# Up projections of a conv feed-forward as 2x2 block products with seven products of block sums

## The reference

```
g, u = split(h @ w_up)               # 1024 -> 2 * 2816
y = (silu(dwconv3(g, w_conv)) * u) @ w_down
```

## Time and profile before

| | us |
|---|---|
| median of 3 runs | 1462.82 |
| lowest, highest | 1462.06, 1465.18 |
| span of the profiled execution | 1461.5 |
| PE busy | 1418.0 (97%) |
| DVE busy | 1003.8 (69%) |
| ACT busy | 521.3 (36%) |
| POOL busy | 85.7 (6%) |

### The profile page before, as it was taken

One profiled execution on the slowest core, in us unless ns is written; L12 is line 12 of the kernel. 1 busy time (PEld: TensorE's weight loads), 2 busy tenths in 40 slices (PEclk: granted clock), 3 DMA queues, 4 the chain that ended last, 5 costly groups with the idle time before them and its releaser, 6 DMA issues.

```text
span 1461.5 us, 20681 instructions
## 1 busy us (share of the span) xinstructions
PE 1418.0 (97%) x7952; PEld 1225.0 (84%) x7952; DVE 1003.8 (69%) x1537; ACT 521.3 (36%) x833; POOL 85.7 (6%) x139
## 2 busy tenths in 40 slices
PE   6999899999999999999999999989999999999998
PEld 3788698889888888888888878868998888888887
DVE  5587988778867666656665688788757555555555
ACT  4342866234222122222121225466445233223321
POOL 0023700000000000000000000350000000000000
PEclk9999999999999999999999999999999999999999
DMA  9643011332643243325333411301022322322324
GB/s 386 278 132 99 1 44 61 130 114 101 200 130 115 88 142 115 106 95 155 118 95 106 138 49 58 115 15 44 15 97 92 101 86 100 100 86 86 114 92 139
DMA packets 42983, 158.62 MB, mean 109 GB/s; under 512 B 5168, under 2 KB 6576, under 8 KB 41776
## 3 DMA queue, kind: packets, MB, share of 16 engines
q1 hardware_dynamic: 42928, 157.87, 32.3%
HBM read 155.76 MB, written 2.10 MB: 108 GB/s over the span
## 4 chain that ended last, share of the span: by engine, by line
PE 84%; DVE 9%; ACT 3%; DMA 2%; issue 1%; SPq 0%; DVEq 0%; ACTq 0%
PE ps L708 67%; PE ps L646 4%; PE ps L647 4%; PE ps L648 4%; DMA ada_step<-in_w_step 1%; DVE w_lo L1373 1%; DVE tmp L1473 1%; PE ps L858 1%; PE ps L660 1%; DVE H_lo L1482 1%; DMA w_raw<-in_w_main 1%; DVE nmax L1687 1%; DVE qn L1660 1%; DVE pt_lo L1488 1%; DVE part_sums L1635 1%
## 5 line engine op out<-in xcount | busy, mean ns | idle before, releaser
L708 PE MATMUL ps<-H_hi,w_hi 128*128 128x512 f32 (+1 forms) x1280 | 449.1, 351 | 4.2 <-DVE H_lo L1482 1.7
L708 PE MATMUL ps<-H_lo,w_hi 128*128 128x512 f32 (+1 forms) x1280 | 447.4, 350 | 0.0
L708 PE MATMUL ps<-H_hi,w_lo 128*128 128x512 f32 (+1 forms) x1280 | 447.1, 349 | 0.0
L1045 ACT ACTIVATE w_hi<-w_raw 128x1024 fp32r<-128x1024 f32 x180 | 187.5, 1055 | 423.3 <-PE ps L708 368.3
L708 PEld LDWEIGHTS ps<-H_hi,w_hi 128*128 128x128 f32 x1280 | 242.3, 189 | 38.3 <-DVE H_lo L1482 3.2
L708 PEld LDWEIGHTS ps<-H_hi,w_lo 128*128 128x128 f32 x1280 | 242.2, 189 | 31.6
L708 PEld LDWEIGHTS ps<-H_lo,w_hi 128*128 128x128 f32 x1280 | 242.3, 189 | 30.8
L1495 DVE SCALAR_TENSOR_TENSOR X<-ps,mod,X 128x512 f32<-128x512 f32 (+1 forms) x296 | 180.8, 644 | 108.5 <-PE ps L708 87.3
L1373 DVE TENSOR_TENSOR w_lo<-w_raw,w_hi 128x1024 fp32r<-128x1024 f32 x180 | 221.1, 1239 | 37.5 <-ACT w_hi L1045 36.4
L708 PE MATMUL ps<-inner_hi,w_hi 128*128 128x512 f32 (+1 forms) x528 | 187.6, 355 | 0.3 <-DVE X L1495 0.3
L708 PE MATMUL ps<-inner_lo,w_hi 128*128 128x512 f32 (+1 forms) x528 | 187.2, 355 | 0.0
(11 more groups left out here) (200 smaller groups left out, 1846.8 us busy)
## 6 DMA issues: line engine op xcount, KB each, us to landing
w_raw<-in_w_main SPq DMA_DIRECT2D x182, 512.0 KB, 3.3
ada_raw<-in_w_ada SPq DMA_DIRECT2D x73, 512.0 KB, 4.1
ada_step<-in_w_step SPq DMA_DIRECT2D x7, 2048.0 KB, 14.6
X<-in_x SPq DMA_DIRECT2D x2, 1024.0 KB, 6.8
cb<-in_cvec SPq DMA_DIRECT2D x2, 1024.0 KB, 7.3
out_x<-X SPq DMA_DIRECT2D x8, 256.0 KB, 4.6
rtab<-in_rope SPq DMA_DIRECT2D x4, 384.0 KB, 7.2
X<-in_ctx SPq DMA_DIRECT2D x2, 512.0 KB, 7.9
```

Of the source, the lines that this page charges most:

```text
L708: ins = pe.matmul(job.ps(a, b), ww[:, wsl], xx[:, xk, a:b], start=first and n == 0, stop=last and n == 2)
L1045: act.activation(w_hi[c % 4][:], w_raw[c % 2][:], ACT.Copy).then_inc(chunk_hi, 1)
```

## The change

Units 1 to 10 of the feed-forward compute their up projections in another way; unit 0 and all of `down` keep their products. The two feature tiles of the gate (and then the two of u) are taken as a 2x2 block product: 2 output tiles by 2 halves of the 1024 input features, times 2 halves of the features by 2 halves of the tokens (384 tokens in layer 0, 256 in layer 1). Instead of eight block products there are seven (Winograd's form), numbered 0 to 6 below; each is 4 feature blocks by three matmuls over half the tokens. A group of seven is called `pair`; a unit is the gate pair, `down` of the unit before, the u pair. In unit 10 both pairs stand before `down`.

Sums of token blocks are made once a layer: POOL adds `hi` and `lo` back together (`whole`, five instructions), DVE makes seven sums (`t_add`) and five `lo` tiles (`t_low`), ACT four `hi` tiles beside the one for `H` (`t_high`). Sums of weight blocks are made in place in the raw chunks by DVE, four of 512 columns for each pair (`weight_sum`), and weights are split in pieces of mostly 512 columns (`block_hi`, `block_lo`, a ring of six blocks).

The running sum of products 0, 2 and 4 stays in one PSUM slot. ACT copies it out after product 0, 2 and 4 (`snapshot`), and PE may not add the next product before that. DVE adds the other products to these copies (`add_part`: part 0 must be done before product 6, which goes over product 3 in PSUM). Taps, silu and value then work from SBUF (`gbuf`, `ubuf`). Loads come as two chunks at a time (`load_ff`, `w_ff`). The tables of layer 1 are loaded behind the feed-forward of layer 0, and three chunks of layer 1's first weights are split in its normalisation, where it were two.

```diff
+            def whole(dst, ks, a):
+                hi, lo = (x[:, ks, a:a + hw].bitcast(F32) for x in H)
+                pool.tensor_tensor(dst[:, :, 0:hw], hi, lo, ALU.add).then_inc(h_sum, 1)
+            Job(JOB["wo", L][15]).ready(pool)
+            pool.wait_ge(h_lo[nn], half(nn))
+            whole(u5_raw, slice(0, 4), 0)
+            whole(t4_raw, slice(4, 8), 0)
+            pool.wait_ge(h_lo[nn], half(nn) + 4)
+            whole(t3_raw, slice(0, 4), hw)
+            pool.wait_ge(h_lo[nn], half(nn) + KD)
+            for n in range(2):
+                whole(u6_raw[n], slice(4 + 2 * n, 6 + 2 * n), hw)
...
-            def up(jn, c, i):
-                for n in range(4):
-                    job = Job(jn + n, i, 24)
-                    pe.wait_ge(chunk_lo, c + n + 1 + 12 * i)
-                    job.open(pe)
-                    for one in turn_about(sg, n):
-                        for kk in range(KD):
-                            last = part(job, [one], slot(c + n), P * kk, H, kk, kk == 0, kk == KD - 1)
-                    job.filled(last)
...
+            def pair(un, z):
+                ab, cd = un.pair_jobs(L, z)
+                for b in range(PAIR):
+                    pe.wait_ge(fw_lo, FF_OPS * L + un.op(z, BLOCK_OP[b]))
+                    if b == 0:
+                        ab.open(pe)
+                    if b == 1:
+                        cd.open(pe)
+                        pe.wait_ge(t_lo, 5 * L + 4)
+                    if b == 2:
+                        pe.wait_ge(snap, 60 * L + un.at(6, 3 * z + 1))
+                    if b == 4:
+                        pe.wait_ge(snap, 60 * L + un.at(6, 3 * z + 2))
+                        pe.wait_ge(t_lo, 5 * L + 5)
+                    if b == 6:
+                        pe.wait_ge(c22, 20 * L + un.at(2, z + 1))
+                    job, o = ((ab, 0), (cd, 512), (ab, 0), (cd, 0), (ab, 0), (ab, 512), (cd, 0))[b]
+                    w = 512 * un.block(z, b)
+                    for r in range(4):
+                        for n, (wx, tx) in enumerate(((0, 0), (0, 1), (1, 0))):
+                            ins = pe.matmul(job.ps(o, o + hw), fw[wx][:, w + P * r:w + P * (r + 1)], operand(tx, b, r),
+                                            start=b in (0, 1, 3, 5) and (r, n) == (0, 0), stop=(r, n) == (3, 2),
+                                            skip_group_check=b in (2, 4, 6))
+                            if b >= 5 and (r, n) == (0, 0):
+                                job.filled(ins)
+                    ins.then_inc(prod, 1)
+            def down(jobs, blocks, ops, tiles, x):
...
+            def unit(un):
+                pair(un, 0)
+                if un.last:
+                    pair(un, 1)
+                down([un.down_job(L, m) for m in range(KD)], [un.down_block(k) for k in range(2)], un.down_op(1), un.at(2, 2), inner)
+                if not un.last:
+                    pair(un, 1)
...
+            def snapshot(un, z, n):
+                act.wait_ge(prod, 140 * L + un.at(14, 7 * z + 1 + 2 * n))
+                z_buf, src = (gbuf, ubuf)[z], un.pair_jobs(L, z)[0].ps(0, hw)
+                if n < 2:
+                    act.activation(z_buf[:, 0, hw * n:hw * (n + 1)], src, ACT.Copy).then_inc(snap, 1)
+                else:
+                    both = z_buf[:, 1, 0:w].rearrange("p (s c) -> p s c", s=2)
+                    act.activation(both, src.unsqueeze(1).to_broadcast([P, 2, hw]), ACT.Copy).then_inc(snap, 1)
+            def unit(un):
+                x, y = un.raw("G")
+                snapshot(un, 0, 0)
+                act.wait_ge(fw_sum, 80 * L + un.at(8, 4))
+                block_hi(un.block(0, 6), x[:, 512:1024])
+                snapshot(un, 0, 1)
+                down = un.raw("D")
+                un.landed(act, L, "D")
+                block_hi(un.down_block(0), down[0][:])
+                snapshot(un, 0, 2)
+                block_hi(un.down_block(1), down[1][:])
+                act.wait_ge(c22, 20 * L + un.at(2, 1))
+                tapped(1, un.at(2, 3), gbuf[:, 1, 0:w])
+                x, y = un.raw("U")
+                un.landed(act, L, "U")
+                act.wait_ge(prod, 140 * L + un.at(14, 6))
+                block_hi(un.block(1, 0), x[:, 0:512])
+                act.wait_ge(prod, 140 * L + un.at(14, 7))
+                block_hi(un.block(1, 1), y[:, 0:512])
+                un.pair_jobs(L, 0)[1].taken(act)
+                tapped(0, un.at(2, 2), gbuf[:, 0, 0:w])
+                for n, t in enumerate((1, 0)):
+                    act.wait_ge(taps, 80 * L + un.at(4 * len(sg), 2 * len(sg) * (n + 1)))
+                    silu(t, (1.0, -1.0)[t])
+                un.down_job(L, KD - 1).ready(act)
+                act.wait_ge(fw_sum, 80 * L + un.at(8, 7))
+                block_hi(un.block(1, 2), x[:, 0:512])
+                block_hi(un.block(1, 3), y[:])
+                block_hi(un.block(1, 5), x[:, 512:1024])
+                act.wait_ge(ff_lo[L], un.at(2, 2))
+                snapshot(un, 1, 0)
+                act.wait_ge(fw_sum, 80 * L + un.at(8, 8))
+                block_hi(un.block(1, 6), x[:, 512:1024])
+                x, y = un.raw("G next")
+                un.landed(act, L, "G next")
+                act.wait_ge(prod, 140 * L + un.at(14, 9))
+                block_hi(0, x[:, 0:512])
+                snapshot(un, 1, 1)
+                block_hi(1, y[:, 0:512])
+                snapshot(un, 1, 2)
+                act.wait_ge(fw_sum, 80 * L + un.at(8, 11))
+                block_hi(2, x[:, 0:512])
+                act.wait_ge(v_done, 20 * L + un.at(2, 1))
+                inner_hi(1, inner)
+                act.wait_ge(prod, 140 * L + un.at(14, 13))
+                block_hi(3, y[:])
+                act.wait_ge(prod, 140 * L + un.at(14, 14))
+                block_hi(5, x[:, 512:1024])
+                act.wait_ge(v_done, 20 * L + un.at(2, 2))
+                inner_hi(0, inner)
...
+            dve.wait_ge(h_sum, 5 * L + 5)
+            dve.wait_ge(t_sum, 7 * L + 1)
+            for n in range(2):
+                t_add(t3r[:, 2 * n:2 * n + 2], u6r[n], 1.0, t3r[:, 2 * n:2 * n + 2])
+            dve.wait_ge(t_sum, 7 * L + 3)
+            for n in range(2):
+                t_add(u6r[n], u6r[n], -1.0, u5r[:, 2 * n:2 * n + 2])
+            dve.wait_ge(t_sum, 7 * L + 5)
+            for n in range(2):
+                t_add(t4r[:, 2 * n:2 * n + 2], u6r[n], -1.0, t4r[:, 2 * n:2 * n + 2])
+            t_low(u5[1][:, :, 0:hw], u5r, u5[0][:, :, 0:hw], 1)
+            dve.wait_ge(t_sum, 7 * L + 7)
+            for n in range(2):
+                t_low(u6_lo[n][:, :, 0:hw], u6r[n], u6_hi[:, 2 * n:2 * n + 2, 0:hw], 2 + n)
+            t_low(t4[1][:, :, 0:hw], t4r, t4[0][:, :, 0:hw], 4)
+            def add_taps(t, tile, src, signal, done, count, last=None):
...
-                ff_value(t, u, c0 + C_FF + 4 + 2 * t, t, 0, 0, 0)
+                g, u = Job(JOB["u0", L] + 2 * t), Job(JOB["u0", L] + 2 * t + 1)
+                if L == 0:
+                    ada_u0(t)(0)
+                add_taps(t, t, g.ps(0, w), ff_conv[L], (2 * len(sg) - 1) * t, t + 1, g)
+                if t == 0:
+                    block_lo(0, x[:, 0:512], 1)
+                    block_lo(1, y[:, 0:512], 2)
+                    weight_sum(x, y, 1, 0, 0)
+                else:
+                    weight_sum(x, y, 1, 0, 2)
+                    block_lo(2, x[:, 0:512], 3)
+                    block_lo(3, y[:], 4)
+                if L == 0:
+                    ada_u0(t)(1)
+                u.ready(dve)
+                dve.wait_ge(ff_silu[L], t + 1)
+                u.last_read(dve.tensor_tensor(ubuf[:, t, 0:w], tmp[t][:, 0:w], u.ps(0, w), ALU.mult))
+                if t == 0:
+                    weight_sum(x, y, 1, 0, 1)
+                else:
...
+            def add_part(un, z, part):
+                z_buf, (ab, cd) = (gbuf, ubuf)[z], un.pair_jobs(L, z)
+                first, second = slice(0, hw), slice(hw, 2 * hw)
+                if part == 0:
+                    dve.wait_ge(snap, 60 * L + un.at(6, 3 * z + 3))
+                    dve.tensor_tensor(z_buf[:, 1, first], z_buf[:, 1, first], cd.ps(512, 512 + hw), ALU.add)
+                    dve.tensor_tensor(z_buf[:, 1, second], z_buf[:, 1, second], cd.ps(0, hw), ALU.add).then_inc(c22, 1)
+                elif part == 1:
+                    dve.wait_ge(prod, 140 * L + un.at(14, 7 * z + 6))
+                    ab.last_read(dve.tensor_tensor(z_buf[:, 0, first], z_buf[:, 0, first], ab.ps(512, 512 + hw), ALU.add))
+                else:
+                    dve.wait_ge(prod, 140 * L + un.at(14, 7 * z + 7))
+                    cd.last_read(dve.tensor_tensor(z_buf[:, 0, second], z_buf[:, 0, second], cd.ps(0, hw), ALU.add))
...
+            def unit(un):
+                x, y = un.raw("G")
+                block_lo(un.block(0, 6), x[:, 512:1024], un.op(0, 5))
+                ada_ff(un, 0)
+                down = un.raw("D")
+                for k in range(2):
```

(41 more changed lines are left out.)

552 lines of the change are left out of this document (389 added, 163 removed).

## The result

The changed kernel takes **1592.2 us** (median of 4 runs, 1591.18 to 1596.94) against 1463.0 of the kernel before in the same session (1462.06 to 1465.18): a ratio of 1.0885, 95% interval 1.0868 to 1.0902. It is slower, as forecast, but by 129 us and not by 81, and 2 us outside the range. The profiled execution has a span of 1589.6 us against 1461.5.

What follows compares the result with a forecast made beforehand. PE's instruction stream was taken to bound the kernel. On the 1461.5 us span, units (+7, +26), starts (+30, +6), unit 10 (+1.6, +4.6) and last downs (+5.4) summed to +81: 1544 us, range 1500 to 1590.

Steps and rivals of the forecast that it cites:

- PE's pace: Units 1 to 10: PE's own matmul time if it never waits, 45.9 us a unit in layer 0, 31.1 in layer 1.
- wait (1): Product 6 of the gate pair waits for the chain after product 4: 2.2 us in layer 0, 2.4 in layer 1.
- Wait (2): Product 2 of the next gate pair waits for DVE, then ACT's copy: 1.2 us in layer 0, 1.75 in layer 1.
- Layer 0's unit: Steady feed-forward unit of layer 0: 45.9 us of PE plus 4.9 of waits, 50.8; nine units cost +7 us.
- wait (3): Product 4 of the u pair waits for DVE's queue, with some at product 6: 1.5 us; layer 1 0.25.
- The clock falls: Rival, 18%: PE's waits lower its clock, 1.7 us once in each of 18 units, +31: 1575 us.
- The start of layer 0: Before unit 1: POOL's sums end at 348.5, then DVE's queue delays PE; costs 30 us, or 36 by POOL's slow row.
- The start of layer 1: Before unit 1: narrower tiles, no modulation; product 6 comes 6 us late (3 to 10).
- Layer 1's units: Steady feed-forward units of layer 1: 31.1 us of PE plus 4.4 of waits, 35.5; nine units cost +26 us.
- The ends: Unit 10 adds 1.6 us in layer 0 and 4.6 in layer 1; the last down 2.7 in each layer.
- Lighter waits: Rival, 17%: waits at product 2 of the gate pair and product 4 of the u pair vanish; 1502 us.
- PE goes at its own pace: Rival, 6%: copies ready in time, PE waits only at the starts (14 + 3 us) and ends (5.4): 1428 us.

Runs made afterwards that it cites:

- the last kernel: The one with the three edits, plus two layer 0 modulation columns moved into the normalisation and, in unit 10, one ACT copy before a tap: 1516.9 us.
- the one with the three edits: Changed kernel with part 0's additions ahead of the second down split, token-block sums on DVE, and ACT's copies earlier: 1518.9 us, ratio 1.0379.

## Why the prediction was wrong

The sign and most of the places were right; the size was 48 us short. Two steps failed: the clock was kept out of the sum, and POOL's additions were priced on POOL with nothing for DVE beside them.

- **PE's pace and wait (1)** stand as worked out. PE alone was put at 45.9 in layer 0, and 46.25 were measured where DVE didn't hold it. Product 6 starts 2.29 us (layer 0) and 2.40 (layer 1) after the matmul before; less PE's own 0.17 and 0.12 these are waits of 2.1 and 2.3 for 2.2 and 2.4. Wait (2) is right in layer 1 (1.84 less 0.12 for 1.75).
- **Layer 0's unit, 50.9 us for 50.8, is luck.** Wait (2) was put at 1.2 and is 0.85 (a gap of 1.02 less 0.17); wait (3) was put at 1.5 and is 0.54 in every second unit, nothing in the others. The clock, which wasn't in the sum, made up for it. A fall costs a unit with six modulation instructions 1.3 us (50.91 against 49.63), and one with seven about 0.6 (51.62 against the 51.02 of unit 1, which is the only one without). Without falls the mean would be 50.3, so by this estimate some 5 of the 7.8 us in that row of the table are the clock's.
- **"The clock falls" was set up as a rival, with 18%, "once in each of 18 units", at 1.7 us.** It came in layer 1 in every unit, at 1.5 us, and in layer 0 in six of nine (0.97). The argument against it, that "the waits here lie further apart" than in rows 9, was the first step that failed: a wait of 2.3 us in each unit did it, and one of 2.5 made by hand did it in five of eight. The waits and their clock had to be in one case, not in two. Even so the rival's own 1575 is 17 us short, mostly for the starts. The Trainium skill (TensorE: Matmul & The Clock Gate, "What's actually happening") names two states of the array's clock, 1.2 and 2.4 GHz; the trace agrees, with 0.50 in the low stretch and 1.00 around it.
- **The start of layer 0, "I take the lower, 348.5, as most of it runs with DVE waiting".** This is the second step that failed. POOL's additions took 15.9 us, inside the bounds of 12.4 and 18.3, but they did not run beside DVE: three of DVE's instructions stood for 9.6 us (3.73 + 3.60 + 3.75 less three times 0.48), and the last H_lo came at 352.49. So POOL ended at 358.16 and not at 348.5, and product 0 and product 6 came 9.4 and 10.0 us later than forecast. Had H_lo come in time, POOL's 15.9 us from 336.40 would have ended at 352.3: by this estimate up to 3.8 of the 9.7 us are the lower bound taken for the addition's own size, and the rest is the hold, for which the forecast had nothing. What follows POOL in the queue was sized rightly (20.4 us to product 0 for 20.7). PE's two waits there, forecast at 14 and about 10 us, are 15.2 and 13.9.
- **The start of layer 1, 6 us for 18.5.** Three instructions of DVE stand for 2.63, 2.47 and 2.67 us in the place of 0.48: 6.3 us. The queue up to product 0 is 2.6 us longer than I worked out, and why stays open. Between products 0 and 6 lie 19.7 us, not some 16, with the clock at 0.74.
- **Layer 1's units, forecast 35.5, measured 37.7:** 1.5 are the clock's, 0.4 are waits in the u pair, and 0.3 aren't placed for certain.
- **The ends** were 2.7 us for the last down (gaps of 2.84 against PE's own 0.2), as forecast; unit 10 of layer 0 cost 3 us more than put, part of it at a clock of 0.94. Between the last down of layer 0 and the end of layer 1's attention, where the third chunk and the tables were put at nothing, 1.4 us were lost; no run shows to which of them, or to the clock, they belong.
- **Rivals.** "Lighter waits" (1502) did not come by itself. Edits of the order made the waits lighter (1545.9 and 1565.6 with one of them each), and the forecast's reading that these waits are places in queues was right. "PE goes at its own pace" was put at 1428 on the condition of short waits; with waits as short as the tried orders make them it is 1519, for DVE's work itself then holds layer 0, and the starts stay.

What the change could bring was small to begin with. In layer 1 it takes by the forecast's prices 1.5 us from a unit of 32.6, and no ordering that was run came under 33.8.

## What to carry over

Price a wait of PE together with its clock: one of 2.3 us in a unit of layer 1 brought another 1.5 us with it, and moving two additions ahead of one split gave back 46 us of 129. When a stretch comes out as forecast, look at its parts too: in layer 0's units two errors cancelled. Before you put work on POOL as free, look at what DVE does in those microseconds: it may stand still for each of POOL's additions, so that here seven microseconds on DVE were cheaper than sixteen "beside" it. Where an exchange of PE's work for DVE's leaves both within 5% of each other, as here (45.9 and 44.5 us), expect to lose the start of the stage too: DVE's preparation had nothing of PE's to hide behind, and the lag was not made good.

## What the hardware showed

- **DVE and POOL.** A DVE instruction with two inputs in SBUF that meets a POOL addition lasts until about its end (3.73, 3.60, 3.75 us for 0.48), and in layer 1 2.63, 2.47 and 2.67. With the additions off POOL none is stretched. The kernel before has it as well, and there I could have read it. DVE's timeline, and under it POOL's, of the kernel before:

```profile
98.71 2.53 DVE L1373 TENSOR_TENSOR w_lo<-w_raw,w_hi 128x1024 fp32r<-128x1024 f32 x1
...
119.60 1.75 DVE L1373 TENSOR_TENSOR w_lo<-w_raw,w_hi 128x1024 fp32r<-128x1024 f32 x1 [0.75 <-ACT w_hi L1045]
...
125.48 1.93 DVE L1489 SCALAR_TENSOR_TENSOR ql_lo<-ps,vec,ql_hi 128x768 fp32r<-128x768 f32 x2
```

```profile
98.45 1.71 POOL L586 TENSOR_TENSOR win_r<-win_a 64x797 f32<-64x797 f32 x1
...
118.75 1.52 POOL L588 TENSOR_TENSOR win_a<-win_p 128x799 f32<-128x799 f32 x1 [15.00 <-issue]
...
124.38 1.89 POOL L594 COPY win_r<-win_a 64x784 f32<-64x784 f32 x1
```

  The split of 1024 columns takes 2.53 and 1.75 us beside POOL, 1.22 elsewhere. It goes the other way too: POOL's addition of 797 columns at 120.35, which starts during the second of these splits, takes 2.38 us, and one of 799 columns just before it 1.52. So the slow row, from which the forecast had its upper bound for POOL, was itself a held one. Two instructions with an input in PSUM, at 125.48, take 0.96 us each beside POOL, the time of such a one alone. The Trainium skill (SBUF — State Buffer, "Who interferes with whom") says this: a DVE instruction with two inputs in SBUF and a POOL instruction that reads SBUF exclude each other for the whole instruction, and the one that starts first wins. The traces agree in the hold, and where one starts clearly first: DVE's 1.75 us at 352.89 started 0.17 ahead of POOL's and was not stretched. Where the rows lie closer they don't tell the order: DVE's at 346.33 starts 0.04 ahead of POOL's at 346.37 and is stretched all the same. I had priced the POOL instruction and not asked this.
- **The clock.** With the same wait of 2.28 us at the same place in layer 1 every unit falls (the kernel after), or five of eight (with ACT's copies first); with 2.5 us by hand five of eight; with 1.4 us, or 1.7 us at product 2 alone, none. With one wait of 2.1 us in layer 0 six of nine units fall in the kernel after, all nine with the sums on DVE, four with ACT's copies first. A wait of 2.0 us in `down` did it once in the last kernel, and never in the one with the three edits. A fall is worth 1.5 us in layer 1 and 0.6 to 1.3 in layer 0. What sets which units fall stays open.
- **More work, less time.** 120 matmuls with no use, put where PE waited, made the kernel 13 us faster.
